# Moving the last two groups of probability transposes behind part of the projection work

## The reference, cut to what matters

```python
# forgetting attention (the fox stage)
s = einsum('bqhd,bkhd->bhqk', qb, k) * scale
s = s + cum_q - cum_k
p = softmax(where(mask, s, -inf), axis=-1)
y_fox = einsum('bhqk,bkhd->bqhd', p, v) * silu(fg)

# latent attention (the mla stage)
s = einsum('bqhd,bkhd->bhqk', qn, k_nope) + einsum('bqhr,bkr->bhqk', qr, k_rope)
p = softmax(where(chunk_mask, s * scale, -inf), axis=-1)
y_mla = einsum('bhqk,bkhd->bqhd', p, v) * silu(mg)
```

## Time and profile before

| | us |
|---|---|
| median of 3 runs | 3626.01 |
| lowest and highest | 3620.32, 3626.83 |
| span of the profiled execution, first to last instruction | 3619.8 |

### The profile page before, as it was taken

The page is one execution under the profiler, slowest core; times in us unless marked ns, Lnnn a source line. Parts: engine busy times, 40 slices in busy tenths (PEclk is TensorE's granted clock), DMA queues, the critical chain, the costliest instruction groups (busy, mean ns, idle before and its releaser), DMA issues. The chain is left out here.

```text
span 3619.8 us, 46994 instructions
## 1 busy us (share of the span) xinstructions
PE 3353.8 (93%) x18342; PEld 2652.9 (73%) x18342; DVE 1792.0 (50%) x3378; ACT 1218.3 (34%) x2265; POOL 1070.2 (30%) x589
## 2 busy tenths in 40 slices
PE   7799897799989899999999989999899999998988
PEld 5478675699878777888888867776666677775667
DVE  1788788655554426554544570335444502344443
ACT  3475566444222302000000131334453213344540
POOL 3133000154444335544534333220112332201112
PEclk9899999799999999999999999999999999999999
DMA  3111100000212114221322113110102211101011
GB/s 117 30 41 29 33 5 1 8 1 22 85 53 64 41 35 142 82 93 58 104 70 67 55 41 101 45 36 12 24 1 82 82 55 49 44 13 18 7 71 70
DMA packets 234301, 179.90 MB, mean 50 GB/s; under 512 B 42945, under 2 KB 219249, under 8 KB 233217
## 3 DMA queue, kind: packets, MB, share of 16 engines
q1 hardware_dynamic: 231376, 176.56, 16.0%
q10 hardware_dynamic: 2736, 0.78, 0.1%
HBM read 159.92 MB, written 16.87 MB: 49 GB/s over the span
## 5 line engine op out<-in xcount | busy, mean ns | idle before, releaser
L1102 DVE SCALAR_TENSOR_TENSOR y_T<-y_T 128x1024 f32<-128x1024 f32 x48 | 137.4, 2914 | 0.1
L881 ACT ACTIVATE I-13450a_hi<-I-13449act_f 128x512 fp32r<-128x512 f32 x22 | 13.5, 633 | 338.5 <-DVE I-13449act_f L890 338.5
L914 DVE TENSOR_TENSOR x_T<-x_T,I-13456p_d 128x512 f32<-128x512 f32 x88 | 60.3, 687 | 126.3 <-PE I-13456p_d L846 126.3
L283 PE MATMUL I-13454p_g<-hf_hi,I-13430w_hi 128*128 128x512 f32 x352 | 108.8, 390 | 3.4 <-POOL hf_lo L523 3.4
L1688 DVE TENSOR_TENSOR I-22508S<-I-22508S,c_causal 128x256 f32<-128x256 f32 x32 | 13.8, 431 | 198.1 <-PE I-22508S L1615 198.1
L283 PE MATMUL I-13455p_u<-hf_hi,I-13431w_hi 128*128 128x512 f32 x352 | 109.0, 391 | 2.3 <-POOL I-13433w_lo L269 2.3
L285 PE MATMUL I-13455p_u<-hf_lo,I-13431w_hi 128*128 128x512 f32 x352 | 109.2, 392 | 0.0
L1688 DVE TENSOR_TENSOR I-16194S<-I-16194S,c_causal 128x256 f32<-128x256 f32 x32 | 13.8, 431 | 192.0 <-PE I-16194S L1615 192.0
L287 PE MATMUL I-13455p_u<-hf_hi,I-13433w_lo 128*128 128x512 f32 x352 | 108.8, 390 | 0.0
L285 PE MATMUL I-13454p_g<-hf_lo,I-13430w_hi 128*128 128x512 f32 x352 | 108.4, 389 | 0.0
L287 PE MATMUL I-13454p_g<-hf_hi,I-13432w_lo 128*128 128x512 f32 x352 | 108.4, 389 | 0.0
(11 more groups left out here) (1390 smaller groups left out, 10176.0 us busy)
## 6 DMA issues: line engine op xcount, KB each, us to landing
y_T<-in_w_ada SPq DMA_DIRECT2D x48, 512.0 KB, 3.5
saved_x<-x_T SPq DMA_DIRECT2D x3, 4096.0 KB, 13.6
I-13428w_raw<-in_w_gate SPq DMA_DIRECT2D x22, 512.0 KB, 4.5
I-13429w_raw<-in_w_up SPq DMA_DIRECT2D x22, 512.0 KB, 4.1
x_T<-saved_x SPq DMA_DIRECT2D x2, 4096.0 KB, 14.5
I-13442d_raw<-in_w_down SPq DMA_DIRECT2D x11, 512.0 KB, 4.9
I-13443d_raw<-in_w_down SPq DMA_DIRECT2D x11, 512.0 KB, 4.9
I-895w_raw<-in_w_in SPq DMA_DIRECT2D x8, 512.0 KB, 3.8
```

What stands on the lines that cost most here:

```text
L283: nc.tensor.matmul(out[h], w_hi[:, k, :], hi(k, h), start=(k == 0), stop=False)
L881: nc.scalar.activation(a_hi[s][:, cols], act_f[:, cols], ACT.Copy).then_inc(a_rounded, 1)
L914: nc.vector.tensor_tensor(x_n, x_n, p_d[n % 2][:, h, :], ALU.add).then_inc(d_added[n % 2], 1)
L1102: self.nc.vector.scalar_tensor_tensor(out=self.raw[s], in0=self.raw[s], scalar=1.0, in1=self.c_row, op0=ALU.mult, op1=ALU.mult, accum_out= ...
```

## The change

The groups of a unit's transposes are parted in two: the first two ("early") and the rest ("late", only units of tile 4 to 7 have any). In a step the early ones stay behind the scores. In the fox stage the half block is parted too: the multiplications of the first two of eight depth tiles (`BETWEEN = 2`, six multiplications) come next, then the late groups, then the other 18 multiplications. In the mla stage the whole half block comes between early and late groups. The waits of a part are those that it had: the wait for the scaled probabilities stands before group 0, the wait for split weights before depth tile 0, and the signal that a half block is done after its last multiplication. Where a step has no projection, the late groups follow the early ones directly. The order on ScalarE, VectorE, GpSimd and SyncE is not touched, nor is the last unit, whose groups are all issued at once behind the loop.

```diff
--- before.py
+++ after.py
@@ -1557,15 +1557,18 @@
         pool.wait_ge(self.rounded, n + 1)
         self.nc.gpsimd.tensor_tensor(lo, raw, hi.bitcast(F32), ALU.subtract).then_inc(self.ready, 1)
 
-    def multiply(self, pe, m, kt, out, hi, lo):
+    def multiply(self, pe, m, kt, out, hi, lo, tiles=None):
         n, h = divmod(m, 2)
         s, part = n % self.slots, slice(h * BANK, (h + 1) * BANK)
-        pe.wait_ge(self.ready, n + 1)
-        for k in range(kt):
+        tiles = range(kt) if tiles is None else tiles
+        if tiles[0] == 0:
+            pe.wait_ge(self.ready, n + 1)
+        for k in tiles:
             self.nc.tensor.matmul(out, self.hi[s][:, k, :], hi[:, k, part], start=(k == 0), stop=False)
             self.nc.tensor.matmul(out, self.hi[s][:, k, :], lo[:, k, part], start=False, stop=False)
             last = self.nc.tensor.matmul(out, self.lo[s][:, k, :], hi[:, k, part], start=False, stop=(k == kt - 1))
-        last.then_inc(self.done, 1)
+        if tiles[-1] == kt - 1:
+            last.then_inc(self.done, 1)
 
 
 class PairedHeads:
@@ -1597,6 +1600,10 @@
     def groups(self, u):
         return (u % NT) // 2 + 1
 
+    def turn_parts(self, u):
+        first = min(2, self.groups(u))
+        return range(0, first), range(first, self.groups(u))
+
     def turns_before(self, u):
         return sum(self.groups(v) for v in range(u)) + 2 * (u // NT + 1)
 
@@ -1615,10 +1622,12 @@
                     last = self.nc.tensor.matmul(out[:, h, a:b], stationary(h, t), moving(h, a, b), start=(n == 0), stop=(n == len(terms) - 1))
         last.then_inc(self.scores_ready, 1)
 
-    def pe_turn(self, pe, u):
+    def pe_turn(self, pe, u, groups=None):
         t, before, ident = u % NT, self.turns_before(u), self.const["c_ident"][:, :]
-        pe.wait_ge(self.scaled, 2 * (u + 1))
-        for g in range(self.groups(u)):
+        groups = range(self.groups(u)) if groups is None else groups
+        if 0 in groups:
+            pe.wait_ge(self.scaled, 2 * (u + 1))
+        for g in groups:
             wait(pe, self.turned_out, before + g - 1)
             for k in range(2 * g, min(2 * g + 2, t + 1)):
                 for h in range(2):
@@ -1722,6 +1731,7 @@
     FIRST = 6
     N_HALVES = 2 * len(columns)
     LAST = PAIRS - 1
+    BETWEEN = 2
     filler = lambda i, t: FIRST + NT * i + t
 
     def filled(i, t):
@@ -1869,8 +1879,9 @@
                     elif t == NT // 2:
                         pe.wait_ge(hb.out, k_at[i] + 2)
                     ph.pe_scores(pe, u, terms(i))
+                    early, late = ph.turn_parts(u - 1) if u > 0 else (range(0), range(0))
                     if u > 0:
-                        ph.pe_turn(pe, u - 1)
+                        ph.pe_turn(pe, u - 1, early)
                     m = filled(i, t)
                     if (i, t) == (NORM, NT - 1):
                         latent_sums(pe)
@@ -1878,7 +1889,11 @@
                         pe.wait_ge(hb.out, m)
                         if i == LAST:
                             pe.wait_ge(l_var_set, 2)
-                        hb.multiply(pe, m, KD, half_of(m), hi, lo)
+                        hb.multiply(pe, m, KD, half_of(m), hi, lo, range(0, BETWEEN))
+                    if late:
+                        ph.pe_turn(pe, u - 1, late)
+                    if m is not None:
+                        hb.multiply(pe, m, KD, half_of(m), hi, lo, range(BETWEEN, KD))
                     if i == LAST and 1 <= t <= len(PARTS):
                         latent_spread(pe, t - 1)
                     if u > 0:
```

## The result

The changed kernel ran at 3604.64 us (median of 4 runs, 3601.02 to 3608.04), the kernel before at 3626.42 in the same session: ratio 0.9943, 95% interval 0.9931 to 0.9956. Six further runs of the changed kernel gave 3608.67 against 3625.60: 0.9953 (0.9940 to 0.9966). So the change takes 17 to 22 us, where I had forecast 5.3 (3620.7, range 3613.5 to 3628.0): right in sign, three to four times too small, and outside the range.

What follows compares the result with a forecast made beforehand. TensorE, busy 94% and 90% in the second block's two attention stages, was taken as the bound. Fox 6.8 + mla 3.0 - clock 4.5 = 5.3 us less, put on the median, gave 3620.7 us, range 3613.5 to 3628.

Steps and rivals of the forecast that it cites:

- The mechanism: Both attention stages: projection between early and late transposes removes a 0.50 us bubble, at 22 places in each stage over two layers.
- The printed 0.25: Wait that the profile row prints before group 2; the prediction took the bubble as 0.85 - 0.35 = 0.50 us instead.
- rival D: The real bubble is only the printed 0.25 us, so the time stays within 2 us of 3626; chance 0.13.
- the price of the switch: Fox stage: cutting the projection after six multiplications adds 2 x 0.095 = 0.19 us, leaving 0.31 a place, 6.8 us over 22.
- Gain per place 0.50 - 0.18 = 0.32: Mla stage: values directly behind transposes cost 0.37 instead of 0.19 us; gain taken as 0.33 a place, 3.0 us both layers.
- Rival B: The switch in the fox stage is free, so fox brings 11.0 us and the time is 3616.5; chance 0.14.
- The clock: Mla pair changes: longer TensorE idle times bring three more falls to 1.2 GHz at 1.5 us each, 4.5 us lost.
- the middle change: Mla stage, middle pair change: idle grows from 2.44 to 3.15 us, so one further clock fall counted in the first layer.
- Rival C: The clock doesn't follow the longer idle times, so 9.8 us are saved and the time is 3616.2; chance 0.15.
- the step with the sums of the latents: Fox pair 2, t = 7, no projection: taken as unchanged, late groups directly behind early ones.
- 2.94 us of slack against 1.05 + 0.31: hidden: Fox t = 7: scaling ends 2.94 us before TensorE comes, so exponentials 1.05 us later and the 0.31 gain cost nothing.
- Rival E: Slower: the clock falls at all five further mla pair changes at 3.0 us each, giving 3631.2; chance 0.08.

## Why the prediction was wrong

Both layers, first trace, from scores to scores, in us, against the terms of the prediction:

| term | predicted | measured |
|---|---|---|
| fox, 20 steps t = 5, 6, 7, 0 | -6.2 | -8.9 |
| fox, from pair 2, t = 7 on | -0.6 | -2.3 |
| mla, 12 steps t = 5, 6 | -4.0 | -5.7 |
| mla, 6 pair changes (t = 7 and t = 0) | +5.5 | +2.1 |
| sum | -5.3 | -14.9 |

**The mechanism was right.** The bubble of 0.50 us, its 22 and 22 places, no wait behind six multiplications, exponentials later by ScalarE's order, the gain of t = 7 in the mla stage lost at t = 0, idle times of 2.3 and 3.2 us there: each is in the rows. The printed 0.25 was not the bubble (rival D is out).

**The step that failed is the price of the switch**, "The cut adds one more of each: 2 x 0.095 = 0.19 us", and its twin in the mla stage, "Gain per place 0.50 - 0.18 = 0.32". Measured, the way into the transposes costs nothing (0.23 to 0.24 us, the step between two multiplications), the late groups themselves pass 0.06 us faster than directly behind a wait, and only the way out costs 0.095. In the mla stage I took the 0.18 from the way out of the transposes (0.37 instead of 0.19) and left out that the way out of the multiplications changes too: into the transposes it is 0.23, where before it was 0.33 to the values (2637.33 to 2637.66 in the earlier trace rows and the line below). And from two transposes to the values it is 0.32 now (2648.12 to 2648.44), not 0.37. So a fox place brought 0.40 to 0.50 us instead of 0.31, and an mla place 0.47 to 0.49 instead of 0.33. The 0.32 that I took from the earlier trace rows was the step to the values, another kind of instruction with its own first wait, and no row showed multiplication to transposes. By the rule of the Trainium skill that the prediction set aside ("TensorE: Matmul & The Clock Gate", "Step-by-step: what each phase is for"), weights of a later multiplication loaded while an earlier one runs, both ways would be hidden. The trace agrees for the way into the transposes, 0.23 to 0.24 us, and not for the way back, 0.32. Rival B was half right.

```profile
2637.33 0.40 PE L1567 MATMUL I-18966half<-h_hi,I-18949w_lo 128*128 128x512 f32 x1
```

Of the 9.6 us between -5.3 and -14.9, the price of the switch makes 2.7 in the fox steps, 1.7 in the mla steps t = 5 and 6, and some 1.8 of the 3.4 at the changes of pairs: with the clock held these would be 0.8 us shorter in sum (six times 0.54 at t = 7, less 2.4 at t = 0), and I had 1.0 longer.

**The clock** was the second size: I counted three further falls at 1.5 us; the first trace has three in all against one before, the second has two, so two or one. That makes the other 1.5 us at the changes of pairs. The price for each was right, the places were not. I was surest of the middle change, as its idle time is the longest. In the eight traces with the moves at t = 7 and nothing in the wait, two layers each, the clock fell 16 times of 16 at the first change (2.32 us idle), twice at the middle one (3.17) and once at the last (2.32 again). So the length of the idle time alone does not tell; what does is open. Rival C was half right too, and that the sum of the falls came near was luck.

**Missed** was the step with the sums of the latents. I wrote, in the section on the change too, that where there is no projection the late groups stand directly behind the early ones; the diff puts the sums between them. That is 0.3 to 1.0 us a layer, of the 1.7 us that the fox stage from pair 2, t = 7 on brought beyond the forecast; the rest of these is clock and the larger gain at t = 0 of pair 3.

**Right by luck** was "2.94 us of slack against 1.05 + 0.31: hidden". Counted to TensorE's need it is true, but the cover of VectorE's scaling ended where GpSimd's split began, 0.36 us before the scaling was over. Three more multiplications cost 0.85 us at each such change, and the fourth group moved behind six more cost 3.4, or 5.0 with a fall of the clock. Rival E did not come.

## What to carry to other kernels

A bubble is the distance between two starts less what the same pair takes without a wait, not the idle time printed before the instruction. The price of a switch between kinds of work is that of exactly this pair in this direction; where no row shows it, keep "nothing" as a likely value and not as an end of the range. And slack is counted up to the first engine that wants something of the late instruction, also if it is no reader of its result: here GpSimd, whose split held VectorE up though neither touched the other's data.

## What the runs showed of the hardware

Two scalings of 128x1024 on VectorE took 1.42 us alone, 3.05 with one operation of GpSimd between them and 5.16 with two. Falls of TensorE's clock from 2.4 to 1.2 GHz at the changes of pairs in the mla stage came behind idle times of 2.32, 2.44, 2.45 and 3.17 us, not behind each, and with the projection first also behind 1.57 (the 9.19 us step) and behind waits of 0.41 and 1.07 with three multiplications between them (the 9.69 us step). A fall cost about 1.5 us. Filling the wait with 8 to 12 unused multiplications of 512 columns, in one trace and six changes, avoided it and delayed nothing. Four transposes directly behind a running multiplication pass at 0.43 us to the next group (2647.69 to 2648.12 in the first trace after), behind a wait at 0.49 (2647.24 to 2647.73 with the projection first):

```profile
2647.69 0.60 PE L1635 MATMUL I-18963PT<-c_ident,I-18967probs 128*128 128x128 f32 x4
2648.12 0.38 PE L1635 MATMUL I-18964PT<-c_ident,I-18967probs 128*128 128x128 f32 x2
2648.44 1.75 PE L1657 MATMUL I-18965O<-x_T 128*64 128x128 f32 x28
```
